# Four turned groups split on GpSimd, sums of diff heads two steps sooner, four norm sums in float32r

## The reference, cut to what matters

```
x = first_block(x):
    h = rmsnorm(x);  qkv = h @ w_qkv
    diff heads (4, width 128):  w = softmax(q1 k1) - lam * softmax(q2 k2);  o = w @ v
    sb heads (8, width 64):     stick-breaking weights from z = q k;        o = a @ v
    o = rmsnorm(o per head) * gain                # "head sums" below
    x = x + rmsnorm(concat(o) @ w_o)
    h = rmsnorm(x);  u = conv3(h @ w_up);  y = (gelu(gate) * val) @ w_down
    x = x + rmsnorm(y)
x = second_block(x):
    x = x + 0.5 * swiglu(rmsnorm(x))              # ffn1
    x = x + hybrid_mixer(rmsnorm(x))              # two kinds of attention
    x = x + 0.5 * swiglu(rmsnorm(x))              # ffn2
    return rmsnorm(x)
```

## Time and profile before

| | |
|---|---|
| median of 3 runs | 1652.62 us (1652.4 to 1652.94) |
| profiled execution | 1652.4 us, span 1650.6 us, granted clock 0.998 |
| PE busy | 1628.0 us, 99% |
| DVE, ACT, POOL busy | 693.2, 672.8, 753.6 us (42, 41, 46%) |
| chain that ended last | PE 81%, DVE 3%, issue 1%, ACT 1%, POOL 1% |

### The profile page before, as it was taken

The page is one execution under the profiler, slowest core; times in us unless marked ns, Lnnn a source line. Parts: engine busy times, 40 slices in busy tenths (PEclk is TensorE's granted clock), DMA queues, the critical chain, the costliest instruction groups (busy, mean ns, idle before and its releaser), DMA issues.

```text
span 1650.6 us, 21039 instructions
## 1 busy us (share of the span) xinstructions
PE 1628.0 (99%) x8108; PEld 1351.2 (82%) x8108; DVE 693.2 (42%) x1399; ACT 672.8 (41%) x1181; POOL 753.6 (46%) x574
## 2 busy tenths in 40 slices
PE   9999999999999999999999999999999999999997
PEld 8788778888888888888888888888888888888886
DVE  7176756874444226311212225555773311112224
ACT  6355645543334234422222324567563422223322
POOL 7424334564444552744445552643114554445550
PEclk9999999999999999999999999999999999999999
DMA  5411102322223221322222222312002322222231
GB/s 204 147 52 52 52 1 102 115 96 96 102 89 103 94 98 56 123 92 101 101 90 102 89 102 90 103 65 78 27 27 90 102 90 102 91 101 99 93 102 51
DMA packets 42115, 147.35 MB, mean 89 GB/s; under 512 B 4768, under 2 KB 5152, under 8 KB 42016
## 3 DMA queue, kind: packets, MB, share of 16 engines
q1 hardware_dynamic: 40680, 143.39, 25.0%
q10 hardware_dynamic: 1336, 2.63, 0.5%
HBM read 142.84 MB, written 3.41 MB: 89 GB/s over the span
## 4 chain that ended last, share of the span: by engine, by line
PE 81%; DVE 3%; issue 1%; ACT 1%; POOL 1%; DMA 0%; DVEq 0%; ACTq 0%; POOLq 0%
PE PS L525 20%; PE PS L526 20%; PE PS L527 20%; PE PS L1099 5%; PE PS L494 4%; PE PS L1110 3%; PE PS L931 2%; PE PS L501 2%; PE PS L906 2%; PE PS L924 1%; POOL w_lo L569 0%; DVE L L1022 0%; DMA stage<-in_weights 0%; PE PS L547 0%; ACT sq L969 0%
## 5 line engine op out<-in xcount | busy, mean ns | idle before, releaser
L569 POOL TENSOR_TENSOR w_lo<-stage,w_hi 128x512 fp32r<-128x512 f32 x524 | 709.4, 1378 | 829.2 <-ACT w_hi L557 828.3
L557 ACT ACTIVATE w_hi<-stage 128x1024 fp32r<-128x1024 f32 x262 | 274.5, 1056 | 509.8 <-DMA stage<-in_weights 507.8
L525 PE MATMUL PS<-H_hi,w_hi 128*128 128x512 f32 x992 | 387.6, 391 | 0.4 <-DVE rcol L1288 0.4
L527 PE MATMUL PS<-H_hi,w_lo 128*128 128x512 f32 x992 | 386.0, 389 | 0.0
L526 PE MATMUL PS<-H_lo,w_hi 128*128 128x512 f32 x992 | 385.9, 389 | 0.0
L525 PEld LDWEIGHTS PS<-H_hi,w_hi 128*128 128x128 f32 x992 | 186.2, 188 | 40.4 <-issue 1.0
L526 PEld LDWEIGHTS PS<-H_lo,w_hi 128*128 128x128 f32 x992 | 186.2, 188 | 39.3 <-issue 1.0
L527 PEld LDWEIGHTS PS<-H_hi,w_lo 128*128 128x128 f32 x992 | 186.2, 188 | 38.6
L525 PE MATMUL PS<-A_hi,w_hi 128*128 128x512 f32 x528 | 205.6, 389 | 0.3 <-DVE A_lo L679 0.2
L694 DVE TENSOR_TENSOR conv<-PS,rstd 128x512 f32<-128x512 f32 x88 | 56.5, 686 | 354.7 <-PE PS L527 338.6
L526 PE MATMUL PS<-A_lo,w_hi 128*128 128x512 f32 x528 | 205.4, 389 | 0.0
(11 more groups left out here) (223 smaller groups left out, 2038.5 us busy)
## 6 DMA issues: line engine op xcount, KB each, us to landing
stage<-in_weights SPq DMA_DIRECT2D x262, 512.0 KB, 3.2
out_t<-Y SPq DMA_DIRECT2D x8, 256.0 KB, 2.0
X<-in_x_t SPq DMA_DIRECT2D x3, 512.0 KB, 8.5
bias_line<-bias_line ACTq DMA_DIRECT2D x1, 1270.0 KB
strip<-bias_line ACTq DMA_DIRECT2D x1, 1024.0 KB, 4.9
stage<-in_weights SPq DMA_DIRECT2D x2, 256.0 KB, 4.6
V<-QF SPq DMA_DIRECT2D x4, 128.0 KB, 2.3
V<-QF SPq DMA_DIRECT2D x4, 127.8 KB, 2.3
```

The lines of the kernel that those rows point to most:

```text
L525: pe.matmul(out, a, h_hi, start=first, stop=False, skip_group_check=skip)
L527: return pe.matmul(out, b, h_hi, start=False, stop=last, skip_group_check=skip)
L557: act.activation(w_hi[:, slot, :], stage[:, slot, :], ACT.Copy).then_inc(hi_done, 1)
L569: lo = pool.tensor_tensor(w_lo[:, slot, cols], stage[:, slot, cols], w_hi[:, slot, cols].bitcast(F32), ALU.subtract)
```

## The change

It has four parts.
- The sum of a diff head (groups 1, 3, 5) goes to the front (`dve0`) of the step in which its squares stand on POOL, and ACT's Ln and Exp one step forward. Those of sb heads stay.
- For the turned groups 0 to 3 (`SPARED`) ACT copies bank 7 to a buffer `turn_f`, two deep, and POOL makes `H_hi` (a copy) and `H_lo` (a subtraction) from it. POOL does this in its steps 42 to 45, ahead of what else stands there. PE's next transposes wait for ACT's copy alone.
- In four of the norms (attn_pre, ffn_pre, ffn1, ffn2) the total is split by ACT (hi) and DVE (lo) and summed by two float32r matmuls. In the three FFNs `pe_stat` comes after unit 4 rather than before it, and ACT makes the next weight units in front of its wait for the sum: two before the total's copy, two after it.
- `ones` is float32r; POOL fills `ident` and copies it to `ones` for that, and zeroes `ident` later.

```diff
+SPARED = 4
+            sq_parts = sb("sq_parts", [P, 2, T], F32R, scope)      # same place as sq
+                turn_f = sb("turn_f", [P, 2, T], ctx=inner)
+                self.parts = self.fold and name != "mix"
+        def act_total(act, n):
+            act.wait_ge(n.added, n.adds)
+            act.activation(total_part(0), n.total, ACT.Copy).then_inc(n.total_hi, 1)
+        def dve_total(dve, n):
+            dve.wait_ge(n.total_hi, 1)
+            dve.tensor_tensor(total_part(1), n.total, total_part(0).bitcast(F32), ALU.subtract).then_inc(n.total_lo, 1)
         def pe_stat(pe, n):
+            if n.parts:
+                pe.wait_ge(n.total_lo, 1)
+                for part in range(2):
+                    mm = pe.matmul(PS[:, STAT, :], ones[:, :], total_part(part), start=(part == 0), stop=(part == 1))
+                mm.then_inc(norm_summed, 1)
+                return
...
-        def act_norm(act, n):
+        def act_norm(act, n, u_up=None):
             for k in range(KC):
                 act_square(act, n, k, X[:, k, :])
+            if n.parts:
+                for u in (0, 1):
+                    act_next(act, u_up + u)
+                act_total(act, n)
+                for u in (2, 3):
+                    act_next(act, u_up + u)
             act_inverse(act, n)
...
-            pe_stat(pe, norm)
             for u in range(4, 2 * FC):
                 ...
                 pe_chunk(pe, (u_up + u) % RING, pair_bank(u // 2) + u % 2)
+                if u == 4:
+                    pe_stat(pe, norm)
...
-            if g >= 1:
-                pe.wait_ge(o_split[b], g)
+            if b == 0 and 1 <= g <= SPARED:
+                pe.wait_ge(o_copied, g)
+            elif g >= 1:
+                wait_turned(pe, b, g - 1)
...
         def act_turn1(act, b, g):
             act.wait_ge(o_turned[b], g + 1)
-            act.activation(turned(b, g)[0], PS[:, 7, :], ACT.Copy).then_inc(o_hi[b], 1)
+            if b == 0 and g < SPARED:
+                if g >= 2:
+                    act.wait_ge(o_pool, g - 1)
+                act.activation(turn_f[:, g % 2, :], PS[:, 7, :], ACT.Copy).then_inc(o_copied, 1)
+            else:
+                act.activation(turned(b, g)[0], PS[:, 7, :], ACT.Copy).then_inc(o_hi[b], 1)
+        def pool_turn1(pool, g):
+            hi, lo = turned(0, g)
+            pool.wait_ge(o_copied, g + 1)
+            pool.tensor_copy(hi, turn_f[:, g % 2, :]).then_inc(o_pool_hi, 1)
+            pool.wait_ge(o_pool_hi, g + 1)
+            pool.tensor_tensor(lo, turn_f[:, g % 2, :], hi.bitcast(F32), ALU.subtract).then_inc(o_pool, 1)
...
+        for g in range(SPARED):
+            at = filled(FILL1, 24 * 12 + turn_steps(g)) + 1
+            hook(at1, "pool", at, lambda pool, g=g: pool_turn1(pool, g))
         for p in range(7):
-            at = groups1[p + 1] + 5
-            hook(at1, "dve", at, dve_head(p))
-            hook(at1, "act", min(at + 1, len(items1) + 1), act_head(p))
+            at = groups1[p + 1] + 4
+            if GROUPS1[p][0] == "diff":
+                hook(at1, "dve0", at, dve_head(p))
+                hook(at1, "act", at + 1, act_head(p))
+            else:
+                hook(at1, "dve", at + 1, dve_head(p))
+                hook(at1, "act", min(at + 2, len(items1) + 1), act_head(p))
...
-            pool.memset(ones[:, :], 1.0 / D).then_inc(const_done, 1)
-            pool.memset(ident[:, :], 0.0).then_inc(const_done, 1)
+            pool.memset(ident[:, :], 1.0 / D).then_inc(ones_filled, 1)
+            pool.wait_ge(ones_filled, 1)
+            pool.tensor_copy(ones[:, :], ident[:, :]).then_inc(const_done, 1)
...
+            act_total(act, n_attn_pre)
             for u in range(5):
                 act_next(act, U_SV + u)
```

More of the change, by code:

```diff
@@ L224, in build @@
         par = sb("par", [P, N_PARAMS])
-        ones = sb("ones", [P, P])
+        ones = sb("ones", [P, P], F32R)
         ident = sb("ident", [P, P])
@@ L231, in build @@
         sb("gap1", [P, 8])
+        with ExitStack() as scope:
+            sq_parts = sb("sq_parts", [P, 2, T], F32R, scope)
         sq = sb("sq", [P, 2, T])
@@ L324, in build @@
         const_done = sem("const_done")
+        ones_filled = sem("ones_filled")
         dve_self = sem("dve_self")
@@ L374, in __init__ @@
                 self.squared = sem(f"{name}_squared")
+                if self.parts:
+                    self.total_hi, self.total_lo = sem(f"{name}_total_hi"), sem(f"{name}_total_lo")
                 self.added = sem(f"{name}_added")
@@ L425, in dve_add, with total_part @@
                               ALU.add).then_inc(n.added, 1)
-        def pe_stat(pe, n):
+        def total_part(part):
+            return sq_parts[:, part, :]
+        def act_total(act, n):
[4 more added lines that the diff above has]
+            dve.tensor_tensor(total_part(1), n.total, total_part(0).bitcast(F32), ALU.subtract).then_inc(n.total_lo, 1)
+        def pe_stat(pe, n):
+            if n.parts:
[4 more added lines that the diff above has]
+                return
             pe.wait_ge(n.added, n.adds)
             if n.fold:
-                pe.matmul(PS[:, STAT, :], ones[:, :], n.total, start=True, stop=True).then_inc(norm_summed, 1)
+                pe.matmul(PS[:, STAT, :], ones[:, :].bitcast(F32), n.total, start=True, stop=True).then_inc(norm_summed, 1)
                 return
             for bank, cols in zip(n.banks, halves()):
-                pe.matmul(PS[:, bank, cols], ones[:, :], n.total[:, cols], start=True, stop=False)
+                pe.matmul(PS[:, bank, cols], ones[:, :].bitcast(F32), n.total[:, cols], start=True, stop=False)
             for k in range(n.adds + 1, KC - 1):
@@ L437, in pe_stat @@
                 for bank, cols in zip(n.banks, halves()):
-                    pe.matmul(PS[:, bank, cols], ones[:, :], sq[:, k % 2, cols], start=False, stop=False)
+                    pe.matmul(PS[:, bank, cols], ones[:, :].bitcast(F32), sq[:, k % 2, cols], start=False, stop=False)
             for half, (bank, cols) in enumerate(zip(n.banks, halves())):
                 pe.wait_ge(n.squared, KC + half)
-                pe.matmul(PS[:, bank, cols], ones[:, :], sq[:, (KC - 1) % 2, cols], start=False,
+                pe.matmul(PS[:, bank, cols], ones[:, :].bitcast(F32), sq[:, (KC - 1) % 2, cols], start=False,
                           stop=True).then_inc(norm_summed, 1)
@@ L446, in pe_warm @@
             for _ in range(count):
-                pe.matmul(PS[:, 0, 0:P], ones[:, :], ones[:, :], start=True, stop=True)
+                pe.matmul(PS[:, 0, 0:P], ones[:, :].bitcast(F32), ones[:, :].bitcast(F32), start=True, stop=True)
         def act_inverse(act, n):
@@ L481, in dve_norm @@
                 dve_add(dve, n, k)
+            if n.parts:
+                dve_total(dve, n)
             if wait:
@@ L1080, in turned, with wait_turned @@
             return (H_hi[:, k, :], H_lo[:, k, :]) if b == 0 else (T_hi[:, k, :], T_lo[:, k, :])
+        def wait_turned(eng, b, g):
+            if b == 0 and g < SPARED:
+                eng.wait_ge(o_pool, g + 1)
+            else:
+                eng.wait_ge(o_split[b], g + 1 - (SPARED if b == 0 else 0))
         def act_turn1(act, b, g):
             act.wait_ge(o_turned[b], g + 1)
-            act.activation(turned(b, g)[0], PS[:, 7, :], ACT.Copy).then_inc(o_hi[b], 1)
+            if b == 0 and g < SPARED:
+                if g >= 2:
[9 more added lines that the diff above has]
+            pool.tensor_tensor(lo, turn_f[:, g % 2, :], hi.bitcast(F32), ALU.subtract).then_inc(o_pool, 1)
         def dve_turn1(dve, b, g):
             hi, lo = turned(b, g)
-            dve.wait_ge(o_hi[b], g + 1)
+            dve.wait_ge(o_hi[b], g + 1 - (SPARED if b == 0 else 0))
             dve.tensor_tensor(lo, PS[:, 7, :], hi.bitcast(F32), ALU.subtract).then_inc(o_split[b], 1)
@@ L1095, in pe_wo1 @@
                 hi, lo = turned(b, g)
-                pe.wait_ge(o_split[b], g + 1)
+                wait_turned(pe, b, g)
                 cols = bass.ts(TURN_ORDER[b][g], P)
@@ L1591, in run @@
                     pool_lo(pool, u)
-            pool.memset(ones[:, :], 1.0 / D).then_inc(const_done, 1)
-            pool.memset(ident[:, :], 0.0).then_inc(const_done, 1)
+            pool.memset(ident[:, :], 1.0 / D).then_inc(ones_filled, 1)
+            pool.wait_ge(ones_filled, 1)
+            pool.tensor_copy(ones[:, :], ident[:, :]).then_inc(const_done, 1)
             pool.memset(epsc[:, :], EPS).then_inc(const_done, 1)
             pool.memset(strip[:, N_DIFF, 0:P], 0.0).then_inc(const_done, 1)
+            pool.wait_ge(const_done, 1)
+            pool.memset(ident[:, :], 0.0).then_inc(const_done, 1)
             pool.wait_ge(const_done, 4)
@@ L1720, in _ @@
             act_next(act, U_WO + KC - 1)
-            act_norm(act, n_ffn_pre)
-            for u in range(4):
-                act_next(act, U_UP1 + u)
+            act_norm(act, n_ffn_pre, U_UP1)
             act_ffn(act, 0, U_UP1, U_DN1, True)
```

(8 more changed lines are left out.)

5 lines of the change are left out of this document (4 added, 1 removed).

## The result

The changed kernel takes 1660.85 us (median of 6, 1659.59 to 1661.07) against 1652.93 (1652.4 to 1654.48): ratio 1.0045, 95% interval 1.0036 to 1.0055, 7.9 us slower. The forecast was 1657.7, 5.1 slower, with a range from 1655.0 to 1662.0. The profiled execution took 1659.59, the lowest of the six; its span is 1657.5 against 1650.6, granted clock 0.996 against 0.998.

The account below looks back on a forecast made before the run. TensorE, busy 1628.0 of 1650.6 us, was taken to bound the kernel. Terms 8.9 - 2.1 - 1.8 + 0.1 = +5.1 on the profiled 1652.4 gave 1657.5, against the median 1657.7; range 1655.0 to 1662.0.

Parts of the forecast that it names:

- wait at item 16's bank: Scores of items 18 and 19 wait for item 16, behind the early sum at step 16: 3.97 us of new PE wait.
- wait at item 28's bank: Scores of items 30 and 31 wait for item 28, behind the early sum at step 28: 4.97 us.
- rival a: PE's clock falls in the new stalls, some 2.7 us per stall: 1660.4 with one, 1663.1 with both; chance 0.13.
- turned groups: Four turned groups on POOL: 2.1 of PE's 3.5 us of waits saved, between 0 and 3.5.
- norm sums: Four norm sums as two fp32r matmuls instead of one fp32: 1.8 us less, from 1.6 to 2.1.
- start: PE's warm-up starts some 0.4 us later because ones needs a copy: cost 0.1, between 0 and 0.5.
- the sum of part 1: Early sums of diff heads at steps 16, 28 and 40: 8.9 us lost together, none at step 40.
- Case (c): Only one of the two waits reaches PE, through another order of POOL's work: 1653.3; chance 0.09.
- case (d): POOL's squares at steps 16 and 28 are in time: early sums cost nothing, 3.8 us won, 1648.8; chance 0.06.
- case (b): POOL is slow with the turned groups, copies at 1.28, and PE's gain goes: 1659.8; chance 0.08.
- the one of `wo(2)`: At the turned groups wo(2) waits 0.35 us for POOL's third group, behind its second and head group 5's products.
- cover: In the FFNs the total's parts are there by 299.7 and PE asks for them at 302.9.

Follow-up runs that it names:

- experiment 3: The changed kernel with 16 and 21 unused float32 matmuls on ones ahead of the scores of items 18 and 30, filling the stalls: 1656.91 us.
- experiment 5: The changed kernel with the early sum for diff group 5 alone; groups 1 and 3 have theirs in the old place: 1648.03 us.
- experiment 4: The changed kernel with GpSimd squaring diff groups 1 and 3 a step sooner, ahead of w_lo and the products; early sums stay: 1647.93 us.
- experiment 8: The kernel before with the float32r norm sums, ScalarE's new order and the new start alone: 1650.47 us.
- experiment 11: experiment 5 with the float32r norm sum of the three FFNs back ahead of unit 4: 1659.66 us.
- experiments 9 and 2: The kernel before with one part each: 9, the turned groups alone, 1650.44 us; 2, the early sums alone, 1665.32 us.
- experiment 10: experiment 4 with six turned groups on GpSimd instead of four, each ahead of all else in its step: 1650.54 us.
- experiment 6: The changed kernel with the sum of head 3 back at its old step, heads 1 and 5 early: 1653.63 us.
- experiment 7: The changed kernel with the sum of head 1 back at its old step, heads 3 and 5 early: 1655.15 us.

## Why the prediction was right, and where its sum was not

The direction, the places and the mechanism of the two stalls held. But 3.9 us of the loss came by a second mechanism, the clock, for which the sum had nothing. Of the steps:

| step | forecast | in the trace | by runs |
|---|---|---|---|
| wait at item 16's bank | +3.97 | 3.84 | one stall: 5.6 with its clock |
| wait at item 28's bank | +4.97 | 4.86 | one stall: 7.1 with its clock |
| taken up later | 0 | -0.7 to -0.8 at 139 | |
| clock behind the stalls | 0 (rival a: 2.7 each) | +1.6 each | +3.9 for both |
| turned groups | -2.1 | -2.0 | -2.1 |
| norm sums | -1.8 | -2.2 | -2.4, with the start |
| start | +0.1 | -0.1, no more than it varies | |

The first two rows of the trace's column are waits; the others compare how late the same matmul starts against before's list, in front of the place and behind it.

- **The stalls.** POOL's order of work could be read from before, and each end of the chain came within 0.15 us of its forecast. With the clock kept up (experiment 3 less experiment 5) they cost 1656.91 - 1648.03 = 8.9 us, the sum of part 1. Case (c), one stall only, is refuted by the two rows; case (d) by POOL's rows, and experiment 4 shows that its condition was the right one.
- **The clock is the term that was missing.** I gave case (a) 0.13 because the longest wait before, 2.33 us, was harmless, and admitted that this says nothing of 5. It was what happened. I had worked out 2.7 us per stall from the warm-up; the runs have 1.8 (5.6 - 3.84) and 2.3 (7.1 - 4.86), in all 3.9 to 4.1, where the 1.8 is what was left after 0.7 had been taken up at 139. The slow stretch was shorter than the warm-up's 5.76 us in most of these traces: 4.0 us (173.16 to 177.2) for the stall with head 3 alone, though 6.7 for head 1 alone. With it the sum would be 5.1 + 3.9 = 9.0 against the 7.9 measured; most of the remainder is what was taken up at 139 and the 0.4 that the norm sums gave beyond their forecast. The Trainium skill, "TensorE: Matmul & The Clock Gate", section "HAM oscillation — how this bites in real kernels", says that long idle gaps put the array back to its lower clock and that each return is paid for. The windows above agree (0.50 behind either stall, 1.00 with the gap filled). It was in the prediction as a rule against the forecast, and deserved more than 0.13.
- **The range held by luck.** The forecast's own range, 1656.3 to 1659.3, did not hold the 1660.85; the wider one did, because it had been reached out towards case (a) with one stall. What happened is case (a) with both stalls, priced at 1663.1 and left out of the range: the time came back under 1662.0 only because each slow stretch was cheaper than its price, 0.8 us was taken up at 139, and the norm sums gave 0.4 more than forecast.
- **Turned groups.** POOL's copy is 0.61 and the subtraction 1.28, as taken from the nearest rows, so case (b) falls. (The prediction gave two different prices for a copy of 1.28: no gain left, at the end of its range and in case (b), and a gain near 1. No run has such a copy.) Turn 2's wait (0.36, forecast 0.35) and the one of item 44's scores (0.69, forecast 0.6) came; the one of `wo(2)`, 0.35, did not: the scores in front of it, at 226.04, waited 0.26 for `stat`. And `wo(0)`, which was to find POOL ready, came 0.3 late. So 2.0 us were gained where 2.1 were forecast, by partly other waits. The Trainium skill, "GPSIMD Engine Reference", section "Engine selection", has one-input operations on GpSimd near line rate and two-input ones at about twice VectorE's time; the new rows agree: 0.61 for the copy, where DVE's sum over one input of the same size (L1312) takes 0.69, and 1.28 for the subtraction against DVE's 0.68 in the earlier trace rows.
- **Norm sums.** 0.46 us for two float32r matmuls, as forecast. Taken over the four norms, the matmuls behind them come 0.4, 0.7, 0.7 and 0.4 us sooner, 2.2 in all, and experiment 8 has the same in its trace. The prediction counted from the float32 sum's own start; in ffn_pre (297.49) it left out that this start itself came 0.40 behind the one of the matmul before it, not 0.23. DVE's subtraction took 1.68, not 0.68; the cover, of which 2.1 us were left against the 3.2 forecast (302.9 - 299.7), hid it. That cover hung on the new place of the sum (experiment 11).
- **Start.** The warm-up started 0.35 later (forecast 0.4), its end met the first operands, and PE's wait of 0.33 vanished. The first product came at 6.98, against 7.08 before. That is no gain of the change: in the nine other traces with the new start it comes at 6.91 to 7.33, and at 6.92 and 7.03 in the two of experiments 9 and 2 with the old one. No cost and no gain is shown.

## What to carry to other kernels

When a wait is moved ahead of work that a saturated engine stands behind, follow the slowest queue's order (here POOL's) and not the step numbers: two steps sooner put a 0.6 us sum 6 us ahead of its input. Price a new stall of TensorE of several microseconds as the stall plus a stretch at half clock behind it, and look for it in the clock column, since PE counts as busy there. And test each part for itself: this change held 4.9 us of gain (1648.03 against 1652.92) under 12.8 us of loss, from two of its three moved sums.

## What the runs showed of the hardware

- The granted clock fell to 0.50 behind waits of PE of 3.84 and 4.86 us; a wait of 2.33 us, at 209.26 before, left it at 1.00. In experiment 10 it also fell behind a wait of 2.50 us, by the times in some executions only; the time of a kernel with such a stall then falls into two groups (1.5 us apart there, 4.2 in experiment 11).
- What the slow stretch cost did not follow the length of the stall. In the profiled executions it was 1.6 and 2.9 us behind the stall of 3.84 (kernel after and experiment 6), 1.6 and 2.0 behind the one of 4.86 (kernel after and experiment 7), 2.8 behind those of 3.14 and 3.16 (experiment 11) and 1.2 behind the one of 2.50 (experiment 10). The moment of the fall varied too: the eight score matmuls right behind the stall of 3.84 took 1.13 us at full clock in the kernel after and 2.08 in experiment 6, where the clock had fallen before the stall ended.
- Small matmuls with no use, 16 and 21 of 128x128 in float32, held the clock at 1.00 and were worth 3.9 us.
- DVE's subtraction for the norm's total takes 0.69 us in the first norm, where POOL is idle, and 1.68, 1.68 and 1.37 in the three FFNs, beside POOL's `w_lo` (306.07 to 310.32 in the first); both read two buffers in on-chip memory. POOL loses too: three of its `w_lo` take 4.25 us beside the subtraction, and 3.81 at 28.86, where DVE does nothing of this kind. Timelines in the kernel after, first norm and third FFN of DVE, and POOL in the first FFN:

```profile
27.86 0.69 DVE L449 TENSOR_TENSOR sq_parts<-rstd,sq_parts 128x512 fp32r<-128x512 f32 x1 [0.70 <-ACT sq_parts L444]
...
1307.36 1.37 DVE L449 TENSOR_TENSOR sq_parts<-rstd,sq_parts 128x512 fp32r<-128x512 f32 x1 [10.31 <-ACT sq_parts L444]
```

```profile
306.07 4.25 POOL L607 TENSOR_TENSOR w_lo<-stage,w_hi 128x512 fp32r<-128x512 f32 x3 [8.61 <-ACT w_hi L595]
```

No experiment took POOL's work away beside it. The Trainium skill, "GPSIMD Engine Reference", section "1. Specifications", says that GpSimd shares its way to on-chip memory with VectorE and that the two get in each other's way when VectorE reads two such inputs; these durations agree with it.
